# Three lanes instead of two for a delta-rule recurrence, with all eight PSUM banks in one rotation

## The reference, cut to what matters

```python
def wkv7_scan(r, decay, k, v, a, b):
    def step(S, inp):
        r_t, w_t, k_t, v_t, a_t, b_t = inp
        sa = jnp.einsum('bhij,bhj->bhi', S, a_t)
        S = S * w_t[:, :, None, :] + sa[..., None] * b_t[:, :, None, :] + v_t[..., None] * k_t[:, :, None, :]
        return S, jnp.einsum('bhij,bhj->bhi', S, r_t)
    ...
def rwkv7_time_mix(...):
    ...
    decay = jnp.exp(-jnp.exp(w_log.astype(jnp.float32)))
    a = jax.nn.sigmoid(a0 + (xa @ a1) @ a2)
    g = jax.nn.sigmoid(xg @ g1) @ g2
    ...
    y = wkv7_scan(heads(r), heads(decay), heads(k), heads(v), -kk, kk * a_h)
    ...
    return (y.astype(h.dtype) * g) @ w_o
```

## Time and profile before

| | us |
|---|---|
| median of the runs | 3565.99 |
| lowest, highest | 3552.95, 3571.19 |
| the profiled execution, its own time | 3558.4 |
| its span from first to last instruction | 3556.6 |
| PE, PEld, DVE, ACT, POOL busy | 3215.9, 2551.1, 1712.3, 1165.2, 142.1 |
| mean granted PE clock, share of full | 0.906 |
| the recurrence, first instruction to first matmul of the next product | 588.6 to 1291.7 |

### The profile page before, as it was taken

The page is one execution under the profiler, slowest core; times in us unless marked ns, Lnnn a source line. Parts: engine busy times, 40 slices in busy tenths (PEclk is TensorE's granted clock), DMA queues, the critical chain, the costliest instruction groups (busy, mean ns, idle before and its releaser), DMA issues.

```text
span 3556.6 us, 38347 instructions
## 1 busy us (share of the span) xinstructions
PE 3215.9 (90%) x15360; PEld 2551.1 (72%) x15360; DVE 1712.3 (48%) x2759; ACT 1165.2 (33%) x1871; POOL 142.1 (4%) x145
## 2 busy tenths in 40 slices
PE   7999798888887889999999999679999978998997
PEld 6888376667675678888788886348888456877886
DVE  5434543454555535434654346765434355335335
ACT  3322133333444333223332223443223243322332
POOL 0000000111111200000000000000000000000000
PEclk9999898676878779999999999679999979998998
DMA  4333131000000023333233332003333410201231
GB/s 127 95 97 100 57 102 33 3 2 3 4 1 14 1 89 95 97 99 95 83 95 95 95 101 80 1 12 95 95 101 95 158 55 1 69 24 45 75 96 55
DMA packets 173894, 234.74 MB, mean 66 GB/s; under 512 B 14201, under 2 KB 111062, under 8 KB 173462
## 3 DMA queue, kind: packets, MB, share of 16 engines
q1 hardware_dynamic: 173718, 232.29, 20.9%
HBM read 228.05 MB, written 4.19 MB: 65 GB/s over the span
## 4 chain that ended last, share of the span: by engine, by line
PE 79%; DVE 12%; ACT 5%; issue 2%; POOL 1%; DMA 1%; SPq 0%; DVEq 0%; ACTq 0%
PE banks L754 59%; PE banks L1179 2%; PE banks L1173 1%; PE banks L847 1%; PE banks L1119 1%; PE banks L909 1%; ACT operand_hi L1423 1%; PE banks L1167 1%; PE banks L885 1%; PE banks L915 1%; POOL operand_hi L2397 1%; PE banks L818 1%; PE banks L913 1%; DVE diff_scores L2138 1%; DVE diff_small L2144 1%
## 5 line engine op out<-in xcount | busy, mean ns | idle before, releaser
L1717 DVE TENSOR_TENSOR weights_lo<-weights_raw,weights_hi 128x1024 fp32r<-128x1024 f32 (+2 forms) x393 | 472.9, 1206 | 1033.3 <-ACT weights_hi L1247 1031.9
L754 PE MATMUL banks<-operand_hi,weights_hi 128*128 128x512 f32 x2208 | 873.8, 396 | 29.5 <-DVE weights_lo L1717 11.6
L754 PE MATMUL banks<-operand_lo,weights_hi 128*128 128x512 f32 x2208 | 866.8, 393 | 0.0
L754 PE MATMUL banks<-operand_hi,weights_lo 128*128 128x512 f32 x2208 | 866.4, 392 | 0.0
L1247 ACT ACTIVATE weights_hi<-weights_raw 128x1024 fp32r<-128x1024 f32 (+2 forms) x393 | 408.0, 1041 | 1093.5 <-PE banks L754 1030.7
L754 PEld LDWEIGHTS banks<-operand_hi,weights_hi 128*128 128x128 f32 x2208 | 419.0, 190 | 124.5 <-issue 19.7
L754 PEld LDWEIGHTS banks<-operand_lo,weights_hi 128*128 128x128 f32 x2208 | 419.2, 190 | 89.3 <-issue 2.4
L754 PEld LDWEIGHTS banks<-operand_hi,weights_lo 128*128 128x128 f32 x2208 | 418.8, 190 | 88.8
L754 PE MATMUL banks<-hidden_ffn_hi,weights_hi 128*128 128x512 f32 x352 | 136.9, 389 | 0.0
L754 PE MATMUL banks<-hidden_ffn_lo,weights_hi 128*128 128x512 f32 x352 | 136.9, 389 | 0.0
L754 PE MATMUL banks<-hidden_ffn_mid_hi,weights_hi 128*128 128x512 f32 x352 | 136.9, 389 | 0.0
(11 more groups left out here) (409 smaller groups left out, 4763.7 us busy)
## 6 DMA issues: line engine op xcount, KB each, us to landing
weights_raw<-in_ffn_w_in_dram SPq DMA_DIRECT2D x352, 256.0 KB, 3.0
weights_raw<-in_ffn_w_out_dram SPq DMA_DIRECT2D x88, 512.0 KB, 3.7
weights_raw<-in_w_in_dram SPq DMA_DIRECT2D x36, 512.0 KB, 3.6
weights_raw<-in_rwkv_w_rkv_dram SPq DMA_DIRECT2D x24, 512.0 KB, 3.8
weights_raw<-in_w_mod_dram SPq DMA_DIRECT2D x24, 512.0 KB, 4.7
weights_raw<-in_w_kv_dram SPq DMA_DIRECT2D x16, 512.0 KB, 3.6
weights_raw<-in_rwkv_w_o_dram SPq DMA_DIRECT2D x8, 512.0 KB, 6.9
weights_raw<-in_diff_w_q_dram SPq DMA_DIRECT2D x8, 512.0 KB, 4.8
```

Of the source, the lines that this page charges most:

```text
L754: mm = nc.tensor.matmul(o, l, r, start=first and t == 0 and job["opens"], stop=last and t == 2, **skip)
L1717: nc.vector.tensor_tensor(ring_lo[0:p, u["slot"], 0:n, 0:w], ring_raw[0:p, u["ring"], 0:n, 0:w], f32(ring_hi[0:p, u["slot"], 0:n, 0:w]), A ...
```

## The change

The 16 items go in turn to three lanes: item i, in the order (0,0), (0,1), (1,0), ..., to lane i % 3. Each lane starts nine steps behind the one before it, and a round is one step of each of three lanes. The lists have 159, 132 and 133 steps; with their starts they end at rounds 159, 141 and 151. The two halves of a pair are now on different lanes, and overlap.

All eight banks turn in one rotation, in the order in which the steps stand in `WKV_ORDER`; a new function `step_of` says which step takes which bank.

The third lane needs tiles. The large ones lie in `third_lane`, which takes the place of `weights_hi` and `weights_lo` in SBUF, and in operand_lo; so nothing is converted during the recurrence, and the two calls of `convert` in the step `lora` go. Values that belong to a pair (decays, rates, gate, the carried state) are held by m % 2 instead of by lane, and some waits are added for the halves that now overlap: DVE waits before writing the carried state until POOL has read that of pair m - 2, POOL waits for the state of half 0, and the last step waits for the gate.

```diff
-WKV_SKEW = 13
+WKV_LANES, WKV_SKEW = 3, 9
...
+        WKV_ITEMS = [(m, half) for m in range(KC) for half in range(2)]
+        lane_of = {item: i % WKV_LANES for i, item in enumerate(WKV_ITEMS)}
+        WKV_ORDER, turns = [], []
+        for lane in range(WKV_LANES):
+            mine = [(lane, *item, step) for item in WKV_ITEMS if lane_of[item] == lane for step in wkv_steps(item[1])]
+            turns.append([None] * (lane * WKV_SKEW) + mine)
+        for i in range(max(len(t) for t in turns)):
+            WKV_ORDER += [t[i] for t in turns if i < len(t) and t[i]]
+        wkv_bank, wkv_before, held, turn = {}, {}, {}, 0
+        for lane, m, half, step in WKV_ORDER:
+            for use, who, event in wkv_uses(half):
+                if step_of(use) == step:
+                    wkv_bank[m, half, use] = b = turn % 8
+                    wkv_before[m, half, use] = held.get(b)
+                    held[b] = (lane_act if who == "act" else lane_dve)[lane], (m, half, event)
                     turn += 1
-        WKV_ORDER = [(0, *w) for w in lane_order[0][:WKV_SKEW]]
-        ahead, behind = lane_order[0][WKV_SKEW:], lane_order[1]
-        for i in range(max(len(ahead), len(behind))):
-            WKV_ORDER += [(0, *w) for w in ahead[i:i + 1]] + [(1, *w) for w in behind[i:i + 1]]
...
         ring_raw = sb("weights_raw", [P, RAW, 2, 512])
+        with ExitStack() as ph:
+            third = sb("third_lane", [P, 2, 12 * HT], on=ph)
...
                 if step == "lora":
-                    for name in LORA2:
-                        for uid in layer[name, m][0]:
-                            convert(uid)
...
-                    dst = L.sbd[:, c + 1] if c < 3 else carry[:, lane]
+                    dst = L.sbd[:, c + 1] if c < 3 else carry[:, m % 2]
+                    if c == 3 and m >= 2:
+                        dve.wait_ge(*done_in(lane_pool, m - 2, 1, "sb0"))
...
                 elif step == "z" and half:
-                    nc.gpsimd.tensor_copy(L.sbd[:, 0], carry[:, lane]).then_inc(*by_pool.by(at("sb0")))
+                    pool.wait_ge(*done_in(lane_dve, m, 0, "s3"))
+                    nc.gpsimd.tensor_copy(L.sbd[:, 0], carry[:, m % 2]).then_inc(*by_pool.by(at("sb0")))
```

104 lines of the change are left out of this document (63 added, 41 removed).

## The result

| | before | after |
|---|---|---|
| median of 4 runs, us | 3568.59 | 3499.88 |
| lowest, highest | 3552.95, 3574.03 | 3491.78, 3512.69 |
| the profiled execution, its own time | 3558.4 | 3507.43 |
| its span | 3556.6 | 3505.6 |
| mean granted PE clock | 0.906 | 0.911 |

The account below looks back on a forecast made before the run. The recurrence was taken as bound by PE's waits and its time at half clock. Savings of 79 us, less 4 for the ends and 5.3 for the conversions, took 3558.4 to 3489 us, range 3415 to 3545.

Parts of the forecast that it names:

- PE's waits and two paces bound the recurrence: Recurrence: PE waits in it and runs a good part at 1.2 GHz; 42.13 us per item before.
- The model of two paces and a share of time: Recurrence before: 36.3 us per item at full clock, 50.9 at half, half the time each, giving 42.4 against 42.13 measured.
- 32 us per item at full clock: Recurrence after: period at full clock, with 3.2 us of waiting where there were 7.5; bounds 28.8 and 37.
- The second rival: Recurrence: an item's first part becomes the bound, 37 us per item at full clock, nothing gained, 3561 us; chance 0.08.
- 47.8 us at half clock, where PE hardly waits: Recurrence after: period per item at half clock, taken between 47.3 and 50.9.
- The share at half clock, 0.40: Recurrence: time share at half clock falls from 0.50 to 0.40 (0.2 to 0.6); period 36.9 us, saving 79 us.
- PE idle under 60 us: Recurrence, profile after: PE's idle time falls from 111 us to under 60.
- the rotation's lag: At `pairs`: if DVE lags, PE waits for a mask, perhaps 1 us per item, 15 us.
- The ends: Tail after the last `pairs`: 37 steps instead of 29 add 4 us (0 to 9); the start is unchanged.
- The conversions: Behind the recurrence: conversions moved to the end make the next product start 5.3 us later.
- The sum: Whole kernel: -79 for the intervals, +4 for the ends, +5.3 for the conversions, -70 us.
- The rotation of banks at nothing: Recurrence: one rotation of all eight banks costs nothing; eight uses lie between two of a bank, as before.

Follow-up runs that it names:

- `norm` late: The changed kernel with DVE doing `norm` (the reciprocal) after the two following steps of the other lanes: 3504.68 us, ratio to before 0.988.
- the reordering: The changed kernel with PE's `decay` after the next lane's step and the first weight unit converted after the operand's first part: 3507.45 us, ratio to before 0.979.
- six joint banks: The changed kernel with its joint rotation over six banks instead of eight: 3497.33 us, ratio to before 0.984.
- eight or twelve in the plain order: The changed kernel with idle matmuls per item: eight at two places 3500.74 us, ratio to before 0.986; twelve at three places 3505.76 us, 0.990.
- the fastest kernel: The changed kernel with late `decay`, early conversion and six idle matmuls ahead of the first doubling after a `norm`: 3459.96 us, ratio to before 0.974.
- skew of 8: The changed kernel with lanes eight steps apart instead of nine: 3521.43 us, ratio to before 0.990.
- own banks: The changed kernel with three, three and two banks tied to its lanes instead of one joint rotation: 3619.03 us, ratio to before 1.020.

## Why the prediction was right, and where it was off

- **PE's waits and two paces bound the recurrence.** Right. All of the gain lies there, and PE's share of the chain rose.
- **The model of two paces and a share of time.** Right. With the half share of 0.5 that was measured, the forecast's own paces give 1/(0.5/32 + 0.5/47.8) = 38.3 us; the trace has 38.25. That it agrees so closely is partly luck, and so was the check before the change (42.4 against 42.13). Both paces were read from one stretch each, for an item of 231 matmul records, while an interval holds 3326/15 = 222 before and 3242/15 = 216 after. Over all the time at one level, 231 records took 34.4 us at full clock, where the prediction had read 36.3, and 60.4 at half clock (1217 records in 318.0 us), where it had 50.9. The records are not all of one size, so these two are estimates.
- **32 us per item at full clock.** Right: 31.1 in three stretches, 31.6 over all. The second rival, 36 or more, fell. But part of the step was there before, since the 36.3 was high. The time didn't go as I worked it out, though: the chain through the first six steps is no longer what sets the pace, and the waits are at masks and state steps.
- **47.8 us at half clock, where PE hardly waits.** Wrong in its reason. The 3.7 us of waiting came from one interval of 50.92; over all the half clock of before PE was idle for 45.2 of 318.0 us. So there was waiting to lose, and 19 of the 30 us of waiting that went, went there. No whole item of common content ran at half clock after the change. Solved for from the period and 31.1, the pace is 0.506/(1/38.25 - 0.494/31.1) = 49.3; by records it is 57.4 (1170 in 290.5 us) against 60.4 before.
- **The share at half clock, 0.40.** This term was mis-sized. It stayed at 0.506. The 15 intervals gained 632.00 - 573.77 = 58 us where 79 were forecast. In the forecast's own paces the share accounts for that: 15 x (38.3 - 36.9) = 21 us. That nothing else is left over rests on the luck just named. The argument was that less waiting would leave fewer falls. What the runs show is that how much PE waits (7.4 us per item before, 5.4 after, 5.2 with `norm` late) hardly moved the share (0.50, 0.51, 0.50), while idle matmuls in a few waits moved it to 0.33, and with the reordering to 0.25, with the waiting nearly unchanged (5.0 to 5.1). I had both halves of the evidence, a fall behind a stretch with waits and 64.90 us at half clock with PE busy, and I gave the first too much weight. The rule of the Trainium skill that I weighed, that continuous matmul work brings the full clock ("TensorE: Matmul & The Clock Gate", section "Why this matters for your kernels"), doesn't hold in so simple a form here: the changed kernel has PE busy for 34.77 of 37.50 us at half clock throughout.
- **PE idle under 60 us.** Missed: 80.9, from 111. I had forecast 3.2 us of waiting per item at full clock, and counted none for a mask. I priced the rotation's lag at perhaps 1 us per item, at `pairs`. It came at the doublings: 22.8 us in 15 intervals, 1.5 per item, with 17.2 more at the state steps. The timeline shows how one of these waits comes of DVE waiting for the root. The number of banks isn't behind them: with six joint banks the doublings wait for the mask nearly as long, 12.1 + 8.9 = 21.0 us.
- **The ends.** Up to ACT's work on the operand, as the earlier trace rows measures it, the tail took 1231.26 - 1173.03 = 58.2 us instead of 56.25, 2.0 more (4 forecast, 0 to 9 as bounds). It is near for a reason that the sum doesn't have: 85 more matmuls stand in it, and its mean clock was 0.85 instead of 0.65. By the order 39 steps follow the last `pairs`, not 37. The start took 13.1 as before (13.3).
- **The conversions.** Right. The next product starts 1238.32 - 1231.26 = 7.06 us after ACT began on its operand, 5.5 more than before; 5.3 were forecast. The rows that answer to the earlier trace rows:

```profile
1230.26 0.42 DVE L2057 TENSOR_TENSOR r<-x_turned,squares 128x256 f32<-128x256 f32 x1
...
1231.26 4.27 ACT L1310 ACTIVATE operand_hi<-r 128x512 fp32r<-128x512 f32 x8 [1.49 <-DVE r L2057]
...
1235.44 1.99 ACT L1289 ACTIVATE weights_hi<-weights_raw 128x1024 fp32r<-128x1024 f32 x2
1236.85 2.35 DVE L1756 TENSOR_TENSOR weights_lo<-weights_raw,weights_hi 128x1024 fp32r<-128x1024 f32 x2
...
1238.32 0.77 PE L796 MATMUL banks<-operand_hi,weights_hi 128*128 128x512 f32 x1 [9.15 <-DVE weights_lo L1756]
```

- **The sum.** Measured in the profiled executions: -58.2 for the intervals, +2.0 for the tail, +5.5 for the conversions, -0.2 for the start, -50.9; the spans differ by 51.0. Forecast: -79 + 4 + 5.3 = -70.
- **The rotation of banks at nothing.** Right for what was asked: against six banks it makes no difference. What I didn't see is that it was needed. With banks of their own the three lanes are 2% slower than the kernel before, and a prediction for that kernel by my steps would have had the wrong sign.

## What to carry to other kernels

Where the engines walk one list, a lane's late result also holds up the other lanes. So after such a change look for the same lateness under another line's name before trying to move it. Where the matrix engine changes between two clocks, forecast with two paces and a share of time, and treat that share as the least certain term: it ran from 0.25 to 0.73 in these kernels and did not follow the waits. Take the two paces from all the time at each level and not from one stretch. Idle matmuls in the waits raised the clock here each time, but not always the speed: six per item with a reordering gave 0.974 against 0.984, eight or twelve in the plain order gained nothing. Whether the six would pay in the plain order, or in the kernel before, was not run.

## What the runs showed of the hardware

- The granted clock of the recurrence didn't follow PE's busy share. At half clock PE was busy for 34.77 of 37.50 us (1085.50 to 1123.00), at full clock for 25.08 of 30.70 (710.00 to 740.70). In the fastest kernel there is a stretch at half clock in which PE is busy throughout (busy counts the modelled ends of matmuls):

```profile
807.80:828.30 20.50, 20.50 (x89) 18.42 (x87) 6.93 (x15) 4.96 (x11) 2.54 (x3) 0.50 0.00 1
```

- Small shifts of the same matmuls change it a lot: the half share was 0.40 with six joint banks, 0.51 and 0.50 with eight, 0.55 with a skew of 8 and 0.73 with own banks, each in one profiled execution, at 5.4 to 6.0 us of idle time per item in all of them.
- The same program on the same chip took 3456.01 and 3512.30 us, at mean clocks of 0.929 and 0.909. A few us of profit in one profiled execution of such a stage prove nothing without the runs beside it.
- 96 matmuls of 128x512 added to the recurrence (466 ns each) and the recurrence got 44.8 us shorter than after the change (607.3 against 652.1), with the reordering of the head sum and of the conversion in the same kernel.
